# Last attention: first head's queries between the second and the third key tile

## What is computed

```python
def shared_kv(h, norm_g, w_kv, knorm_g, cos, sin):
    kv = (rms_norm(h, norm_g) @ w_kv).astype(jnp.float32)
    k, v = jnp.split(kv, 2, axis=-1)              # 4 heads x 128 each
    k = apply_rope(rms_norm(k, knorm_g), cos, sin)
    return k, v

def dilated_layer(h, k, v, norm_g, w_in, qnorm_g, w_out, cos, sin):
    q, z = jnp.split(rms_norm(h, norm_g) @ w_in, [B_QW], axis=-1)
    q = apply_rope(rms_norm(q, qnorm_g), cos, sin)   # 3 groups x 4 heads x 128
    for g, (window, dilation) in enumerate(DILATED_GROUPS):
        o_g, l_g = dilated_window_attention(q[:, :, g], k, v, window, dilation)
    wts = jax.nn.softmax(jnp.stack(lses, axis=0), axis=0)
    o = jnp.einsum('gbsh,gbshd->bshd', wts, jnp.stack(outs, axis=0))
    y = o.reshape(Bsz, S, B_VW) * jax.nn.silu(z)
    return y @ w_out                                 # added to the residual h
```

## Time and profile before

| | |
|---|---|
| median of 3 runs | 1422.5 us |
| the profiled execution | 1422.82 us |
| its span (first to last instruction) | 1420.8 us |
| TensorE busy | 98% |
| VectorE, ScalarE, GpSimd busy | 59%, 42%, 12% |
| mean granted clock | 0.998 |
| the stage of the change (k0 to the last piece) | about 1179 to 1354 us of the span |

### The profile page before, as it was taken

How to read it: one execution, slowest core, us unless ns; L and a number is a source line. 1 busy time by engine, 2 the same in 40 slices (tenths; PEclk the granted TensorE clock), 3 DMA queues, 4 the chain that set the end, 5 groups by cost and what they waited for, 6 DMA issues and landing times.

```text
span 1420.8 us, 17484 instructions
## 1 busy us (share of the span) xinstructions
PE 1397.1 (98%) x6892; PEld 1138.4 (80%) x6892; DVE 838.2 (59%) x1245; ACT 602.9 (42%) x921; POOL 165.5 (12%) x124
## 2 busy tenths in 40 slices
PE   7999999999999999999999999999999999999898
PEld 5777777878888888888888888787778888888686
DVE  5556565745343797624776365645464657687774
ACT  5254433433235554423444255434353544344461
POOL 3300010212212300000000221000002111211030
PEclk9999999999999999999999999999999999999999
DMA  6221322222352333332333324421134333221141
GB/s 231 80 83 52 98 63 75 71 64 91 103 164 88 133 105 104 106 102 83 95 101 119 95 71 137 132 60 60 60 104 149 89 104 107 75 60 46 45 140 68
DMA packets 37265, 135.39 MB, mean 95 GB/s; under 512 B 4400, under 2 KB 5056, under 8 KB 36672
## 3 DMA queue, kind: packets, MB, share of 16 engines
q1 hardware_dynamic: 37184, 134.28, 29.8%
HBM read 127.97 MB, written 6.29 MB: 94 GB/s over the span
## 4 chain that ended last, share of the span: by engine, by line
PE 94%; DVE 2%; ACT 1%; DMA 1%; issue 0%; SPq 0%; POOL 0%; DVEq 0%; ACTq 0%; POOLq 0%
PE ps L203 93%; PE ps L207 1%; DMA cv<-in_cvec 1%; ACT WH L187 1%; DMA raw<-in_wall 1%; SPq L210 0%; DVE TT L162 0%; DVE WL L150 0%; ACT SS L200 0%; DVE SS L174 0%; POOL SQS L150 0%; DVE HL L162 0%; DVE PB L174 0%; DVE TH L150 0%; DVE PB L162 0%
## 5 line engine op out<-in xcount | busy, mean ns | idle before, releaser
L203 PE MATMUL ps<-HH,WH 128*128 128x512 f32 x1088 | 439.6, 404 | 9.3 <-DVE WL L150 8.9
L203 PE MATMUL ps<-HH,WL 128*128 128x512 f32 x1088 | 425.2, 391 | 0.0
L203 PE MATMUL ps<-HL,WH 128*128 128x512 f32 x1088 | 424.5, 390 | 0.0
L150 DVE TENSOR_TENSOR WL<-raw,WH 128x1024 fp32r<-128x1024 f32 x222 | 283.2, 1280 | 78.5 <-ACT WH L187 77.3
L187 ACT CAST WH<-raw 128x1024 fp32r<-128x1024 f32 x222 | 231.5, 1044 | 147.9 <-PE ps L203 130.0
L203 PEld LDWEIGHTS ps<-HH,WH 128*128 128x128 f32 x1088 | 204.9, 188 | 59.2 <-DVE WL L150 8.9
L203 PEld LDWEIGHTS ps<-HH,WL 128*128 128x128 f32 x1088 | 204.6, 188 | 44.3
L203 PEld LDWEIGHTS ps<-HL,WH 128*128 128x128 f32 x1088 | 205.0, 188 | 41.6 <-issue 1.7
L150 POOL TENSOR_TENSOR SQS<-SQS,SQ 128x512 f32<-128x512 f32 x54 | 83.3, 1543 | 743.0 <-ACT SQ L200 727.8
L203 PE MATMUL ps<-PH,WH 128*128 128x512 f32 x424 | 168.7, 398 | 1.1 <-DVE TT L150 1.1
L203 PE MATMUL ps<-PH,WL 128*128 128x512 f32 x424 | 165.7, 391 | 0.0
(11 more groups left out here) (216 smaller groups left out, 1456.8 us busy)
## 6 DMA issues: line engine op xcount, KB each, us to landing
raw<-in_wall SPq DMA_DIRECT2D x222, 512.0 KB, 3.6
kept<-PW SPq DMA_DIRECT2D x2, 2048.0 KB, 9.2
PWR<-kept SPq DMA_DIRECT2D x2, 2048.0 KB, 7.7
X<-in_xT SPq DMA_DIRECT2D x8, 256.0 KB, 5.9
X<-in_xT SPq DMA_DIRECT2D x4, 512.0 KB, 5.5
out_T<-X SPq DMA_DIRECT2D x8, 256.0 KB, 2.0
pe<-in_pT SPq DMA_DIRECT2D x2, 512.0 KB, 4.4
DM<-in_dm SPq DMA_DIRECT2D x1, 640.0 KB, 4.2
```

The costliest lines, as they stand in the source:

```text
L150: return self.put(None if self.e is None else self.e.tensor_tensor(out, x, y, op))
L203: return self.put(None if self.e is None else self.e.matmul(out, l, r, start=start, stop=stop, skip_group_check=True))
```

## The change

Queries of head 0 are projected after k1 and before k2, and the attention is put on `side` there. Their three tiles get memory of their own (`QT2`, over `PH` tiles 8 to 10), so that they needn't wait for "k read", while the other nine stay over the input of the keys. The inputs of the query projection (`HH`, `HL` tiles 4 to 7) are made two at a time behind k0 and k1. The attention's rate is 3.6. The weights' layout and GpSimd's list follow.

```diff
--- before.py
+++ after.py
@@ -597,7 +597,8 @@
         PB = at("PB", [P, T], F32, ar + 35840)
         PT = at("PT", [P, T], F32, ar + 37888)
         OB = at("OB", [P, 4, T], F32, ploff)
-        QT = [at("QT0", [P, 8, T], F32, phoff), at("QT1", [P, 4, T], F32, ploff + 4 * T * 4)]
+        QT = [at("QT0", [P, 8, T], F32, phoff), at("QT1", [P, 1, T], F32, ploff + 4 * T * 4),
+              at("QT2", [P, 3, T], F32, phoff + 8 * T * 4)]
 
         RC = sm[:, 80:84]
         psum = ctx.enter_context(nc.psum_tensor("ps", [P, 8, 512], F32))
@@ -653,7 +654,9 @@
             return [sm[:, o + 4 * q:o + 4 * q + 4] for q in range(5)]
 
         def qt(h, g):
-            half, k = divmod(3 * h + g, 8)
+            if h == 0:
+                return QT[2][:, g, :]
+            half, k = divmod(3 * h + g - 3, 8)
             return QT[half][:, k, :]
 
         def q_rs(h):
@@ -1122,21 +1125,25 @@
             p.mark("ple 0")
             p.tokens4([("vt", t) for t in range(4)], H_kv, [SB[2], SB[3], p.next_bank(), p.next_bank()], early=True)
             p.mark("kv")
-            for h in range(4):
+            def k_proj(h):
                 p.tile(("k", h), H_kv)
                 p.rope(("k", h), pe_rope_k(p, h), 3)
-            p.mark("k read")
 
             def q_proj(h):
                 for g in range(3):
                     p.tile(("q", h, g), H_b)
                     p.rope(("q", h, g), pe_rope_q(p, h, g), 3 if g == 2 else 2)
 
+            for h in range(2):
+                k_proj(h)
             p.op = p.next_bank()
             p.mp.remove(p.op)
             q_proj(0)
-            p.rate = 3.9
+            p.rate = 3.6
             p.side.append(attend())
+            for h in range(2, 4):
+                k_proj(h)
+            p.mark("k read")
             for h in range(1, 4):
                 q_proj(h)
             def until(h):
@@ -1269,7 +1276,8 @@
             name = ("q", h, g)
             u, gn = qt(h, g), c("qnorm")
             v_turned(v, name, u, ps(*name), gn, S.act, "rope sq", name)
-            v.wait_ge(S.pe, "mark", "k read")
+            if h:
+                v.wait_ge(S.pe, "mark", "k read")
             v.scalar_tensor_tensor(u, ps(*name), gn, CS[:, 0, :], MUL, MUL).then_inc(("rope u", name), free(name))
             yield
             if g == 2:
@@ -1875,21 +1883,26 @@
             v.mark("kv")
             for t in range(4):
                 v_low(v, "b", t, "norm_b", HH, HL)
-            for h in range(4):
+            def k_proj(h):
                 v.tile(8)
                 rope_in(h)
-                v_low(v, "b", 4 + h, "norm_b", HH, HL)
-            v.mark("k read")
-            query_eps()
+                for m in range(4 + 2 * h, 6 + 2 * h) if h < 2 else ():
+                    v_low(v, "b", m, "norm_b", HH, HL)
 
             def q_proj(h):
                 for g in range(3):
                     v.tile(8)
                     v.rope(("q", h, g), v_rope_q(v, h, g), 3 if g == 2 else 2)
 
+            for h in range(2):
+                k_proj(h)
+            query_eps()
             q_proj(0)
-            v.rate = 3.9
+            v.rate = 3.6
             v.side.append(attend())
+            for h in range(2, 4):
+                k_proj(h)
+            v.mark("k read")
             for h in range(1, 4):
                 q_proj(h)
             def gated(h):
@@ -2492,20 +2505,25 @@
                 a.activation(VT[:, t, :], ps("vt", t), ACT.Copy, scale=RC[:, t:t + 1]).then_inc(("vt", t), free("vt", t))
                 a.wait_ge(S.pe, "mark", "ple 0")
                 a_high(a, "b", t, "norm_b", HH, S.dve, "x kv", t)
-            for h in range(4):
+            def k_proj(h):
                 a.tile(8)
                 a.rope(("k", h), a_rope_k(a, h), 3)
-                a_high(a, "b", 4 + h, "norm_b", HH, S.dve, "x kv", 4 + h)
-            a.mark("k read")
+                for m in range(4 + 2 * h, 6 + 2 * h) if h < 2 else ():
+                    a_high(a, "b", m, "norm_b", HH, S.dve, "x kv", m)
 
             def q_proj(h):
                 for g in range(3):
                     a.tile(8)
                     a.rope(("q", h, g), a_rope_q(a, h, g), 3 if g == 2 else 2)
 
+            for h in range(2):
+                k_proj(h)
             q_proj(0)
-            a.rate = 3.9
+            a.rate = 3.6
             a.side.append(attend())
+            for h in range(2, 4):
+                k_proj(h)
+            a.mark("k read")
             for h in range(1, 4):
                 q_proj(h)
             def gated(h):
@@ -2673,7 +2691,7 @@
             g_sum(g, "p0")
             g_sum(g, "kv")
             g.mark("kv")
-            for name in [("k", h) for h in range(4)] + [("q", h, i) for h in range(4) for i in range(3)]:
+            for name in [("k", 0), ("k", 1)] + [("q", 0, i) for i in range(3)] + [("k", 2), ("k", 3)] + [("q", h, i) for h in range(1, 4) for i in range(3)]:
                 next(g_rope(g, *name))
             g.mark("attended")
             g_sum(g, "p1")
@@ -2893,11 +2911,13 @@
     ple(0)
     w = i["w_kv_2"]
     wide(w, 512, 512)
-    form(w, 0, 4)
-    w = i["w_in_b_2"][0]
+    wk, w = w, i["w_in_b_2"][0]
+    form(wk, 0, 2)
     for h in range(4):
         for g in range(3):
             form(w, (g * 4 + h) * P)
+        if h == 0:
+            form(wk, 2 * P, 2)
     form(w, 1536, 4)
     side_by_side(*((i["w_out_b_2"][0], m * P) for m in range(3)))
     form(i["w_out_b_2"][0], 3 * P, 5)
```

## The result

The changed kernel takes 1434.0 us (median of 4 runs, 1433.29 to 1434.7) beside 1422.7 for the kernel before: ratio 1.0083, 95% interval 1.0071 to 1.0095. It is 11.3 us slower, where 8.3 were forecast; 1434.0 lies inside the range. The profiled execution took 1434.7 us, its span 1432.7.

What follows compares the result with a forecast made beforehand. TensorE, busy 98% of the span, was taken as the bound, so only its pauses count. Terms 2.5 + 5.5 + 0.3 = +8.3 us on the profiled 1422.8 gave 1431.1, median 1430.8, range 1423.5 to 1437.

Steps and rivals of the forecast that it cites:

- The place of the loss: Head 1's scores still wait for q(1,2): only pieces 0 to 3 come earlier, by two tiles; pieces 4 to 15 end later.
- First term: At q(1,2), TensorE waits for q(1,0)'s bank: VectorE's 31.9 us against 29.4 us, a pause of 2.5 us.
- The stands laid out for DVE: Before q(1,0)'s turning, DVE waits 0.8 us for first exponentials, 1.5 for k2's row, 2.8 for k3's root.
- Second term: In z1, piece 10's weights stand behind z0's gating: 13.4 us chain against TensorE's 7.9, a new pause of 5.5 us.
- Third term: Last pieces: pauses for copies of 10 and 11 shrink by 1.6 us, the end grows by 1.9: net +0.3 us.
- The clock: The 1.7 us dip behind the last pauses stays; a second behind the new pause would add as much, only in the range.
- The first: Faster because pauses behind z0 go, if the 13.4 us chain is under 7.9: 1413.8 us, half gives 1418; chance 0.08.
- The second: No change, as both new pauses, at q(1,0)'s bank and z0's gating, are covered: 1422 to 1425 us; chance 0.15.
- The third: Five table switches on the two chains each hold ACT a second load's length, 6.4 us more: 1437 us; chance 0.05.

Runs made afterwards that it cites:

- the slow start: Changed kernel with the previous kernel's lists from head 1's first scores on, plus rate 2.2 instead of 3.6 up to q(1,2): 1422.42 us, ratio 1.0001.
- The kernel with one step more: Changed kernel with one more attention step on every engine between tile z0 and its gating, at rate 3.6: 1431.72 us, ratio 1.0067.
- the one at the old rate: Changed kernel with its rate put back from 3.6 to 3.9, all else as changed: 1431.23 us, ratio 1.0063.
- the one with the old list: Changed kernel with rate 3.9 and counter set behind q(1,2), so lists from head 1's first scores match the kernel before: 1426.77 us, ratio 1.0029.
- the rate alone: Kernel before the change with only its rate set from 3.9 to 3.6, tiles in their old order: 1429.88 us, ratio 1.0056.
- no root: Changed kernel with ScalarE copying scaled sums instead of taking square roots for the third and fourth key tiles: 1431.07 us, ratio 1.006.
- piece 11 left as before: Changed kernel using waiting steps for values and turnings only at pieces 3 and 7, one step left empty behind piece 8's scores: 1426.44 us, ratio 1.0029.
- That with the spent steps used and head 0 early: Changed kernel with waiting steps before pieces 4, 8, 12 given values and turnings, rate 2.4 until q(1,2), then 4.0: 1425.3 us, ratio 1.0024.

## Why the prediction was right, and what it missed

**The place of the loss: right.** "What doesn't move decides": head 1's scores stayed where they were, so the early start could only help pieces 0 to 3. The first scores of head 1 came 5 us later and not earlier, and the slow start shows that the early one is worth nothing (ratio 1.0001). The waits and the loads named beforehand came: a wait for `QT` of 2.2, one for `PB` of 5.2, 34 table loads.

**First term, 2.5 us: right, with one wrong cause in it.** It is 2.2 in the waits and 2.4 by starts. The stands laid out for DVE were 0.8, 1.5 and 2.8; measured are 0.77, 2.14 and 2.89. The `PB` that meets GpSimd took 1.42. Without the roots the wait is 0.7, so a load was needed for most of it, as the working had it. But it was one load and not three: the working charged k2's row with the two around its root, and that stand is 2.14 us without them too, since the row waits for PE. So it was luck that its size came near. A short wait of 0.5 for `PB` at 1232.4 was not foreseen.

**Second term, 5.5 us: right.** 5.2 in the waits, 5.3 by starts without the slow clock. The kernel with one step more shows its cause, the kernel before at rate 3.6 that it doesn't need the early start.

**Third term, +0.3 us: right in its order, too high in its size.** The copy of piece 14 does stand behind the exponentials and the cast, and PE waits for it. But it waits 3.6 us where 4.6 were forecast. The end was put at 6.8 and is 6.8 by luck: 2.0 of it are the half clock, which the term did not contain, and without them it is 4.8, no more than before. The copies of pieces 10 and 11 gave back all 2.2 us where 1.6 had been taken. The term is thus some -2.4 at full clock.

**The clock: mis-sized, and this is the step that failed.** The prediction let the dip of 1.7 us stay and put a second one into the range alone. There are three: 0.76 over 7 us, 0.62 over 9 and 0.66 over 10. At full clock the pauses come to 0.6 + 2.4 + 5.3 - 2.4 = 5.9 us of the 11.9 between the two profiled executions (0.6 is the short wait for `PB`). By the same instructions at both clocks the three dips hold PE up by 1.7, 2.4 and 2.8 us, 5.2 more than the one before; 0.8 us are left over. So the clock is nearly half of the loss, where the sum had it at nothing, and the third term was too high by half as much. The sum came within 3 us because these two errors offset each other. The earlier trace rows had the warning: a dip stood behind pauses of 5.0 us in all, so a single pause of 5.5 was likely to bring one. One dip each for the two new pauses, at the 1.7 us of the old one, would have made the sum 1434.2, but with the third term still wrong.

**Rivals.** The first failed at its point: the chain was longer than the way of PE, not shorter. The second failed: neither wait was covered. The third, a table switch twice as long, would have given 1437 and left a stand of over 4 us at k3's root; it was 2.89.

**What stays open.** Which pause brings a dip. The 2.2 us wait for `QT` was followed by one in the changed kernel, in the one at the old rate and in the one with the old list, but not in the one with a step more, whose trace has the same wait. The slow start has nearly the waits of the kernel before at the end, and its profiled execution shows no dip there. Each of the four traces with a wait of 5 us (the change, the rate alone, no root, piece 11 left as before) has a dip at it, of 3 to 7 us at half clock.

## What to carry to other kernels

Before giving a stage an earlier start, find what its second part waits for; if that doesn't move, only the first part gains, and steps that wait are steps lost. In a list that is dealt out by a rate, changing the rate or the remainder moves every later step, and the cost sits at single places: a small instruction that others wait for, set behind a root, a cast or a gating, cost 1.5 us (k3's root) to 5 us (z0's gating) here. So change the places and not the rate, and compare against a kernel whose lists are the same except at that place. When a pause of some 5 us is predicted on TensorE, put a dip of its clock into the sum too, and for one of 2 us put it into the range. Read a pause by starts at full clock, or the dip is counted in it.

## What was not expected of the hardware

- A dip costs as much as a small pause: in the kernel with the old list, a wait of 2.2 us was followed by a clock of 0.72 over 6 us, 1.7 us lost; in the one with a step more the pauses at the end, of 2.7 us at most, came with 0.50 over 10 us, as this row of its stretches shows.

```profile
1353.00:1363.00 10.00, 8.36 (x27) 6.89 (x28) 4.18 (x8) 3.36 (x6) 0.00 (x0) 0.50 0.00 0
```

- Whether a pause brings a dip varies between executions of one kernel. That with the spent steps used and head 0 early ran five times at a mean granted clock of 0.999 in 1424.0 to 1425.3 us, and four times at 0.996 or 0.997 in 1426.4 to 1427.7 us: about 2 us hang on it, more than several of the edits tried here. The kernel before varies too: in the executions beside these experiments, 40 at a mean clock of 1.000 have a median of 1421.9 us and 33 at 0.998 or 0.999 one of 1422.5. The dip at its end, which the prediction took as given, is in the one execution that was profiled.
